# A query projection's slabs loaded into free buffers, and four more row gathers let in beside it

## The reference

```python
merged = gates[:, :, 0, :] * branch_conv + gates[:, :, 1, :] * branch_ssm
x = x + merged @ w_out[l]
h = rmsnorm(x, norm_ffn[l])
x = x + peer(h, peer_w_q[l], peer_sub_keys[l], peer_u[l], peer_v[l])
...
def block(xb):                                       # 128 tokens
    q = (xb @ w_q).reshape(128, 8, 2, 128)
    s = jnp.einsum('thcd,hcnd->thcn', q, sub_keys)   # 8 heads, 2 halves, 128 keys
    s_top, i_top = lax.top_k(s, 16)
    ...                                              # 16 x 16 candidates a head
    best, pos = lax.top_k(cand, 16)
    expert = jnp.take_along_axis(cand_idx, pos, axis=-1)
    gates = jax.nn.softmax(best, axis=-1)
    u_sel = u_tab[expert]; v_sel = v_tab[expert]
    act = jax.nn.gelu(jnp.einsum('td,thkd->thk', xb, u_sel))
    return jnp.einsum('thk,thkd->td', gates * act, v_sel)
```

## Time and profile before

| | us |
|---|---|
| runs before, median of 3 | 2504.44 (2503.66 to 2505.58) |
| the profiled execution | 2503.76 |
| its span | 2501.9 |
| busy in the span: PE / DVE / POOL / ACT | 2154.1 / 1613.7 / 670.4 / 611.5 |
| q0 (gathers), share of 16 DMA engines | 51.7% |
| q1 (slabs and the rest) | 23.2% |

### The profile page before, as it was taken

How to read it: one execution, slowest core, us unless ns; L and a number is a source line. 1 busy time by engine, 2 the same in 40 slices (tenths; PEclk the granted TensorE clock), 3 DMA queues, 4 the chain that set the end, 5 groups by cost and what they waited for, 6 DMA issues and landing times.

```text
span 2501.9 us, 24448 instructions
## 1 busy us (share of the span) xinstructions
PE 2154.1 (86%) x9666; PEld 1479.6 (59%) x9666; DVE 1613.7 (65%) x2420; ACT 611.5 (24%) x967; POOL 670.4 (27%) x524
## 2 busy tenths in 40 slices
PE   9999999999999999999977777777777877777775
PEld 8888887888889989988842222223222322222232
DVE  7757687688989895564786766674444444444444
ACT  4345555422154524432120010000101000000000
POOL 0000000000000000000575555455544554544441
PEclk9999999999999999999989999999999999999999
DMA  6544444534445444555999999999999999999997
GB/s 230 188 168 169 168 167 146 199 145 152 152 152 180 158 157 160 187 187 191 421 392 421 422 421 422 421 422 421 422 421 421 422 422 422 421 422 422 422 421 301
DMA packets 103504, 747.97 MB, mean 299 GB/s; under 512 B 11616, under 2 KB 11616, under 8 KB 12896
## 3 DMA queue, kind: packets, MB, share of 16 engines
q0 software_dynamic: 73728, 536.90, 51.7%
q1 hardware_dynamic: 29376, 209.20, 23.2%
q10 hardware_dynamic: 288, 0.31, 0.0%
HBM read 744.28 MB, written 2.10 MB: 298 GB/s over the span
## 4 chain that ended last, share of the span: by engine, by line
PE 53%; DMA 36%; DVE 4%; POOL 4%; issue 2%; ACT 1%; DVEq 0%; POOLq 0%; ACTq 0%
PE ps L504 14%; PE ps L464 13%; DMA slots<-in_peer_v,slots 10%; DMA weight_raw<-in_peer_v,slots 8%; PE ps L507 7%; DMA operand<-in_peer_v,slots 7%; PE ps L745 5%; DMA rows_high<-in_peer_v,slots 4%; DMA slots<-in_peer_u,slots 4%; PE ps L488 4%; PE ps L484 4%; PE ps L485 4%; DMA operand<-in_peer_u,slots 2%; POOL weight_raw L439 1%; POOL slots L439 1%
## 5 line engine op out<-in xcount | busy, mean ns | idle before, releaser
L745 PE MATMUL ps<-slots 128*128 128x512 f32 x736 | 341.8, 608 | 116.1 <-DMA slots<-in_peer_v,slots 116.1
L1129 DVE TENSOR_TENSOR weight_low<-weight_raw,weight_high 128x2048 fp32r<-128x2048 f32 x146 | 334.1, 2289 | 119.7 <-ACT weight_high L759 119.6
L504 PE MATMUL ps<-operand_parts,weight_high 128*128 128x512 f32 x1504 | 372.4, 400 | 7.6 <-DVE operand_parts L1381 3.5
L745 PE MATMUL ps<-weight_raw,slots 128*128 128x512 f32 x608 | 282.1, 609 | 103.1 <-DMA weight_raw<-in_peer_v,slots 88.0
L1621 DVE SCALAR_TENSOR_TENSOR slots<-slots,work 128x2048 f32<-128x2048 f32 x100 | 228.7, 2292 | 199.0 <-DMA slots<-in_peer_u,slots 198.8
L745 PEld LDWEIGHTS ps<-slots 128*128 128x128 f32 x736 | 134.4, 192 | 322.2 <-issue 236.4
L504 PEld LDWEIGHTS ps<-operand_parts,weight_high 128*128 128x128 f32 x1504 | 281.4, 191 | 69.1 <-issue 5.0
L759 ACT ACTIVATE weight_high<-weight_raw 128x2048 fp32r<-128x2048 f32 x146 | 278.6, 1908 | 97.4 <-PE ps L507 95.2
L1078 ACT ACTIVATE slots<-ident,slots 128x128 f32<-128x128 f32 x242 | 85.5, 395 | 815.0 <-PE ps L745 512.3
L422 POOL IOTA slots<- 128x16 f32 x1 | 0.1, 145 | 1043.5 <-DVE slots L1507 1043.5
L745 PEld LDWEIGHTS ps<-weight_raw,slots 128*128 128x128 f32 x608 | 111.8, 193 | 273.3 <-issue 190.6
(11 more groups left out here) (230 smaller groups left out, 2651.7 us busy)
## 6 DMA issues: line engine op xcount, KB each, us to landing
weight_raw<-in_w_in SPq DMA_DIRECT2D x120, 1024.0 KB, 4.8
weight_raw<-in_w_out SPq DMA_DIRECT2D x32, 1024.0 KB, 4.9
weight_raw<-in_peer_w_q SPq DMA_DIRECT2D x16, 1024.0 KB, 6.9
weight_raw<-in_conv_w_out SPq DMA_DIRECT2D x8, 1024.0 KB, 4.8
weight_raw<-in_ssm_w_val SPq DMA_DIRECT2D x8, 1024.0 KB, 4.8
weight_raw<-in_ssm_w_gate SPq DMA_DIRECT2D x8, 1024.0 KB, 5.0
residual_t<-in_x SPq DMA_DIRECT2D x4, 512.0 KB, 5.8
out_y<-work SPq DMA_DIRECT2D x4, 512.0 KB, 5.3
```

What stands on the lines that cost most here:

```text
L504: nc.tensor.matmul(out, high[:, k, :], o_parts[:, :, place(k), :], start=(k == order[0]), stop=False)
L745: mm = nc.tensor.matmul(ps_v[:, c, :], diag[:, n % 16, :], rows[b][:, c * 512:(c + 1) * 512], start=False, stop=False, skip_group_check=True)
L1129: v.tensor_tensor(w_low[:, s % NSLAB, :], w_raw[:, s % NSLAB, :], w_high[:, i % NHIGH, :], ALU.subtract).then_inc(w_low_ready, 1)
```

## The change

Three slabs of w_q, numbers 4, 5 and 6, get a buffer of their own in columns of `slots` that are free by then (columns 24 to 31, 32 to 39 and 8 to 15, that is rows 4 and 5 and the latter of the two last rows). SP issues them within the w_out2 loop, after its slabs 8, 10 and 12, the first behind a wait on `o_low_ready` (the vector work that last reads these columns). `weight_raw` carries the other 13 slabs. `slab_before` counts from 9 in place of 6. `EARLY_PICKS` is 32 and not 28, still over seven buffers, of which rows 4 and 5 are first used at s = 7 and s = 9, once tiles 4 and 5 are done. One softmax on DVE stands at another u row (34, before 33), since the constant beside it grew.

```diff
 EARLY_ROWS, MORE_ROWS = 7, 6
+EARLY_ORDER = (0, 1, 4, 2, 5, 3, 6)
+PRELOADED = (4, 5, 6)
-EARLY_PICKS = 4 * EARLY_ROWS
+EARLY_PICKS = 32
...
 def slab_before(s):
-    return min(6 + (s - UNPACED) // 2, 15)
+    return min(PRELOADED[-1] + 3 + (s - UNPACED) // 2, 15)
 def row_of(s):
+    if s < 5:
+        return (0, 1, 2, 3, 6)[s]
     if s < EARLY_PICKS:
-        return s % EARLY_ROWS
+        return EARLY_ORDER[(s - 5) % EARLY_ROWS]
...
+        w_q_early = [slots_f[:, n * T:(n + 8) * T].rearrange("p (k n) -> p k n", k=KD) for n in (24, 32, 8)]
...
             for t in range(4, 16):
                 load(w_out2, t, TILE_OUT2 + t + 1)
+                if t % 2 == 0 and 0 <= (t - 8) // 2 < len(PRELOADED):
+                    n = (t - 8) // 2
+                    if n == 0:
+                        sp.wait_ge(o_low_ready, O_OUT2 + KD)
+                    sp.dma_start(w_q_early[n], w_q[PRELOADED[n]]...).then_inc(q_landed[n], 16)
             for t in range(16):
-                load(w_q, t, TILE_WQ + t + 1)
+                if t not in PRELOADED:
+                    load(w_q, t, TILE_WQ + t + 1)
...
                 if UNPACED <= s < EARLY_PICKS:
-                    slab = SLAB_WQ + slab_before(s)
+                    slab = SLAB_WQ + slab_before(s) - len(PRELOADED)
                     pool.wait_ge(raw_landed[slab % NSLAB], 16 * (slab // NSLAB + 1))
...
                 if USES[s] > 0:
                     pool.wait_ge(row_free[b], USES[s])
+                elif b in (4, 5):
+                    pool.wait_ge(proj_done, TILE_WQ + b + 1)
...
-                if n == 0:
+                early = PRELOADED.index(t) if tile0 == TILE_WQ and t in PRELOADED else None
+                if early is not None:
+                    pe.wait_ge(q_landed[early], 16)
+                elif n == 0:
...
-                if g == EARLY_PICKS + 5:
+                if g == EARLY_PICKS + 2:
                     softmax(1)
```

More of the change, by code:

```diff
@@ L312, in build @@
         val_gated, merged = sem("val_gated"), sem("merged")
+        q_landed = [sem(f"q_landed{n}") for n in range(len(PRELOADED))]
         picks_ready, best_ready, best_exp, dots_ready, gelu_ready, w_ready, diag_ready = (
@@ L391, in _ @@
                 load(w_out2, t, TILE_OUT2 + t + 1)
+                if t % 2 == 0 and 0 <= (t - 8) // 2 < len(PRELOADED):
+                    n = (t - 8) // 2
+                    if n == 0:
+                        sp.wait_ge(o_low_ready, O_OUT2 + KD)
+                    sp.dma_start(w_q_early[n], w_q[PRELOADED[n]].rearrange("p (k n) -> p k n", k=KD)).then_inc(q_landed[n], 16)
             for t in range(16):
-                load(w_q, t, TILE_WQ + t + 1)
+                if t not in PRELOADED:
+                    load(w_q, t, TILE_WQ + t + 1)
             sp.wait_ge(picks_ready, len(HEAD_PARTS) + 1)
@@ L458, in tile @@
                 w = w_raw[:, (len(slabs) - 1) % NSLAB, :].rearrange("p (k n) -> p k n", k=kts)[:, :, n * P:(n + 1) * P]
+                w = [w[:, k, :] if early is None else w_q_early[early][:, k, :] for k in range(kts)]
                 pe.wait_ge(proj_freed, tile0 + t + 1)
@@ L463, in tile @@
                         pe.wait_ge(*ready(k))
-                    mm = nc.tensor.matmul(ps_p[:, t % PSLOTS, :], w[:, k, :], operand[:, k, :], start=(k == order[0]),
+                    mm = nc.tensor.matmul(ps_p[:, t % PSLOTS, :], w[k], operand[:, k, :], start=(k == order[0]),
                                           stop=(k == order[-1]))
```

## The result

| | before | after |
|---|---|---|
| median, us | 2504.05 (2501.91 to 2505.58, 4 runs) | 2523.27 (2522.21 to 2524.05, 4 runs) |
| profiled execution, us | 2503.76 | 2524.05 |
| its span, us | 2501.9 | 2522.1 |
| DMA rate over 1175 to 1310 us, GB/s | 407 | 317 |

The ratio is 1.0078, with a 95% interval of 1.0066 to 1.009. The page of the kernel after shows the place at once: in its forty slices of 63 us the DMA share, 9 tenths or more from slice 20 on before, is now 7 and 8 tenths in slices 20 and 21, and 9 again behind.

What follows compares the result with a forecast made beforehand. From about 1174 us the DMA engines' bytes set the end. Holes of 26.6 us, less 2.7 of today and 7.5 for three slabs, give 16.4; restart times give 14.9; 15 was taken: 2519 us, range 2511 to 2524.

Steps and rivals of the forecast that it cites:

- The first hole: DMA idle from about 1194.3 until slab 11's bytes at 1208.6, with gathers from 7 on held back: 14.3 us.
- The second and third: DMA idle until gather 7's bytes at 1214.3, 3.2 us, and until slab 13's at 1223.4, 1.6 us.
- 17 transfers at 2.49 us: From 1223.4, slabs 13 to 15 and gathers 9 to 22: 42.3 us plus 0.7, ending at 1266.4.
- How soon a slab lands: Slab time from issue to landing: 4.8 us alone, 9.3 us beside a full queue; the middle was taken.
- Dot 22: DVE's dot on gather 22 ends about 1269.3: 0.6 us for landing and 2.3 for DVE after 1266.4.
- The restart: After dot 23 ends at 1288.5, gather 30 is issued at 1288.7, with first bytes at 1290.6.
- The fourth hole: DMA idle from 1283.8 to 1290.6, as gather 30 waits for dot 23 behind DVE's selection: 6.8 us.
- The break of today: DMA time lost in the kernel before, over 1267.5 to 1275: 2.7 us.
- The loads at nothing: Loading slabs 4 to 6 in the w_out stage costs nothing; without cover, 2.5 us for each of three.
- the stream never runs dry: Rival: from 1175 on, three loads leave the full stretch and the break at 1268 closes; 2494 us, chance 0.05.
- only the first holes count: Rival: DVE's selection is hidden, so the 6.8 us hole before 1290.6 is gone; 2512 us, chance 0.07.
- the early loads are not hidden: Rival: early loads delay w_out slabs, PE waits up to 2.5 us for each; 2526 us, chance 0.03.

Runs made afterwards that it cites:

- The kernel with both edits: Changed kernel without slab waits for the early gathers and with DVE's selection for heads 2 and 3 taken apart; 2495.26 us, ratio 0.9967.
- the split run: Changed kernel, slab waits kept, with DVE's selection for head 2 after dot 9, head 3 after dot 13, expert numbers after 17, softmax after 19; 2517.29 us.

## Why the prediction was right, and what was mis-sized

The direction, the mechanism and the places held. The time was 4.3 us over the forecast of 2519: inside the stated range of 2511 to 2524, but 0.3 us beyond the forecast's own bounds of 2513 to 2523. Its errors lie in terms for which those bounds made no allowance, so that the range still held it is in part luck. Step by step:

- **The first hole** (forecast 14.3 us from 1194.3 to 1208.6). Gather 7 was issued at 1213.23, behind slab 11 issued at 1207.92. The share is 0.10 in 1194 to 1208, and 0.01 in 1196 to 1208. Right.
- **The second and third** were forecast at 3.2 and 1.6 us. The share is 0.03 in 1212 to 1214.5, and in 1223 to 1223.5 it is 0.17. Both are there; the second of them is shorter than I had it.
- **17 transfers at 2.49 us** from 1223.4 to gather 22. This term was mis-sized. The stream ended at about 1286.6 after gather 29, so by bytes gather 22 was through at 1286.6 - 17.4 = 1269.2, not at 1266.4. In the 45.8 us between, the share is 0.99, so hardly any time was idle, but the rate is 391 and not 421 GB/s: 2.69 us for each of 17 transfers. The slow parts are those with few transfers in hand, 323 GB/s in 1223.5 to 1230.5 (share 0.96) and 320 in 1247.5 to 1252.5 (0.91); in 1230.5 to 1240, with about four in hand at its start, it is 417. I had priced all by the row of the full stream, and allowed for idle time alone. Why a short queue is slow, no run shows.

```profile
1223.40:1269.20 45.80, 44.55 (x222) 39.21 (x220) 30.42 (x31) 7.33 (x14) 28.07 (x17) 1.00 0.99 391
```

- **How soon a slab lands** was left between 4.8 and 9.3 us. Measured from SP's issue to POOL's next gather: slab 13 in 5.0 (1222.63 to 1227.67), slab 12 in 9.0, slab 14 in 10.3 (1229.54 to 1239.80), slab 15 in 8.3. Slab 14, beside four queued gathers, fell outside my bounds.
- **Dot 22** ended 4.5 us after its transfer was through by bytes, and not 2.9. The dot itself is as forecast; the 0.6 us for landing was a term without a row, and it was 2.3. The DMA view of the kernel after has gather 22 (issued at 1259.83) landing after 11.7 us, at 1271.5, and dot 22 starts at 1271.50. The first row is of that view, the others are dots 20, 22 and 23 on DVE's timeline:

```profile
operand<-in_peer_u,slots POOLq DMA_INDIRECT x1, 11.7
...
1266.91 2.29 DVE L1639 SCALAR_TENSOR_TENSOR rows_high<-rows_high,work 128x2048 f32<-128x2048 f32 x1
...
1271.50 2.29 DVE L1639 SCALAR_TENSOR_TENSOR operand<-operand,work 128x2048 f32<-128x2048 f32 x1
...
1290.54 2.28 DVE L1639 SCALAR_TENSOR_TENSOR slots<-slots,work 128x2048 f32<-128x2048 f32 x1
```

- **The selection** took 16.8 us (1273.72 to 1290.54), forecast 17.0. Right.
- **The restart** after dot 23 (ended at 1292.8) took 3.9 us to the first bytes at about 1296.7, forecast 2.1. POOL's issue of gather 30 lasted 2.24 us, where that of the row it was priced by lasted 0.94. The first bytes are in this half microsecond, read as the one of before at 1270.50:

```profile
1296.50:1297.00 0.50, 0.00 (x0) 0.00 (x0) 0.50 (x1) 0.00 (x0) 0.50 (x1) 0.50 1.33 197
```

- **The fourth hole** is with this 1296.7 - 1286.6 = 10.1 us, forecast 6.8 (1286.6 is by bytes; the last packets come until 1289).
- **The sum**: the restart at 1296.7 in place of 1290.6 gives (1296.7 - 1270.7) - 4.98 = 21.0 us; the span moved by 20.2. The form of the sum was right. Its terms together were 6.1 us short: 2.8 for the transfers, 1.6 for dot 22, 1.8 for the restart, and -0.1 for the selection with dot 23.
- **The break of today** was read as 2.7 us from the share. By the GB/s of the same two rows it is 3.5 x (1 - 82/421) + 4 x (1 - 344/421) = 3.55 us: the share counts an engine as busy also while it moves less.
- **The loads at nothing** held: the share rose to 0.60 in the w_out stage, and PE's last scores are 0.26 us later.
- **The rivals.** The one by which the stream never runs dry needed gather 7 by 1192; it came at 1213. The kernel with both edits comes near that rival, at 2495.26 us where 2494 was forecast for it, though its stream still has gaps. The rule of the Trainium skill ("DMA: Bandwidth & Descriptors", section "Rules for kernel authors": issue early, wait late) points to the same time, and the runs bear it out for the slabs themselves in part: 3.3 us of the 7.5, from 2498.51 to 2495.26. It says nothing on what the loads leave behind them: three tiles fed from elsewhere free no raw buffer, so the next slab comes 31.16 us later. The rival in which only the first holes count fell with the fourth hole, and the one in which the early loads are not hidden fell with PE's 0.26 us.

## What to carry to other kernels

When some transfers are taken out of a ring of buffers, ask what recycles the ring: the loads behind them bunch up, and every wait that counts by those loads moves with them, here a pacing wait of quite another queue. Taking that wait out was tried; counting it by other slabs, so that gathers 7 and 8 wait for an earlier one, was not. When a saturated DMA stream sets the time, count the bytes that it moves per stretch, not its busy share alone; one row a kernel accounted for nine comparisons. And once more transfers are let in, look at who frees their buffers: a stretch of vector work is hidden only while the buffers in hand hold longer than it lasts.

## What the runs showed that I had not expected

How long POOL's issue of a gather takes depends on DVE. In the kernel before, from 1165 to 1500 us, 71 of the 75 issues that began while no dot was in progress took about 0.94 us, also beside the small instructions of a selection; all 58 that began during a dot took longer, 1.9 us in the middle. In the changed kernel, behind the fourth hole, the start of one issue follows the last by 2.21 to 2.22 us, which is DVE's step from dot to dot (POOL's timeline of the kernel after):

```profile
1298.36 1.91 POOL L453 DMA_INDIRECT weight_raw<-in_peer_u,slots  x1 [0.30 <-issue]
1300.58 1.91 POOL L453 DMA_INDIRECT weight_raw<-in_peer_v,slots  x1 [0.30 <-issue]
1302.79 1.91 POOL L453 DMA_INDIRECT weight_raw<-in_peer_u,slots  x1 [0.30 <-issue]
```

So a queue that has run empty fills by no more than 0.28 us of work per gather (2.49 - 2.21) as long as DVE catches up. That is a likely reason why stretches behind a hole move less than 421 GB/s (375 in the split run); no run tests it by itself. The Trainium skill, "Advanced Engine Details and Errata", section "VectorE Performance Modes", notes that VectorE's second SBUF port is shared with GpSimd, and that GpSimd instructions and VectorE instructions in a two-port mode block each other. No row here shows whether a dot runs in such a mode, and no run takes this apart from other causes, so the cause stays open.
